# A transformer chain in split fp32: high and low parts of x side by side in the column chunks, and the first two chunks of five stages with token tiles stationary

## What is computed

```python
x = layer_norm(ALPHA * x + dsa_mixer(x))             # sparse attention
x = layer_norm(ALPHA * x + squared_relu_mlp(x))      # jnp.square(relu(x @ w_up)) @ w_down, 1024 -> 4096
x = layer_norm(ALPHA * x + gla_mixer(x))             # q, k, v, r, a_low = split(x @ w_in); 4 heads
x = layer_norm(ALPHA * x + squared_relu_mlp(x))
x = layer_norm(ALPHA * x + mla_mixer(x))             # latents = x @ w_dqkv first
x = layer_norm(ALPHA * x + swiglu_ffn(x))            # (silu(g) * u) @ w_down, 1024 -> 2 x 2816
x = x + sigmoid(x @ ple_w_gate) * (p[0] @ ple_w_proj)
x = layer_norm(ALPHA * x + hgrn2_mixer(x))           # q, f, v, gate = split(x @ w_in); 8 heads
x = layer_norm(ALPHA * x + swiglu_ffn(x))
x = x + sigmoid(x @ ple_w_gate) * (p[1] @ ple_w_proj)
# layer_norm: (x - mean) * rsqrt(mean((x - mean)**2) + 1e-5) * g + b
# gla_mixer: log_a = log_sigmoid(a_low @ w_a2 + b_a) / 16 decays the state, q and k are scaled by it
```

## Time and profile before

| | us |
|---|---|
| median of 3 runs | 1422.44 |
| lowest, highest | 1420.70, 1422.44 |
| the profiled execution | 1421.68 |
| its span (first to last instruction) | 1419.9 |
| TensorE busy in it | 1311.9 (92%) |
| VectorE, ScalarE busy | 843.4 (59%), 572.2 (40%) |
| mean granted TensorE clock, as a share of full rate | 0.967 |

### The profile page before, as it was taken

One profiled execution on the slowest core, in us unless ns is written; L12 is line 12 of the kernel. 1 busy time (PEld: TensorE's weight loads), 2 busy tenths in 40 slices (PEclk: granted clock), 3 DMA queues, 4 the chain that ended last, 5 costly groups with the idle time before them and its releaser, 6 DMA issues.

```text
span 1419.9 us, 19097 instructions
## 1 busy us (share of the span) xinstructions
PE 1311.9 (92%) x8181; PEld 1185.4 (83%) x8181; DVE 843.4 (59%) x1146; ACT 572.2 (40%) x652; POOL 82.6 (6%) x198
## 2 busy tenths in 40 slices
PE   6978899997998899999878899999999988999997
PEld 5867799996987799997767899998898877999996
DVE  5584855557566755557645754447667658554465
ACT  5452344443633344443342433444451233433333
POOL 2450000000000000000230000000000000000000
PEclk9999999999999999999889999999999999999999
DMA  7410655554632455554330655555553325555542
GB/s 247 147 60 2 207 178 185 198 181 145 189 129 90 156 197 181 185 198 144 119 119 8 226 190 178 185 195 191 172 164 119 119 67 178 180 192 192 179 152 86
DMA packets 128757, 221.06 MB, mean 156 GB/s; under 512 B 6904, under 2 KB 97040, under 8 KB 128672
## 3 DMA queue, kind: packets, MB, share of 16 engines
q1 hardware_dynamic: 125648, 209.83, 44.1%
q0 software_dynamic: 3024, 10.01, 2.4%
HBM read 218.77 MB, written 1.05 MB: 155 GB/s over the span
## 4 chain that ended last, share of the span: by engine, by line
PE 80%; DVE 12%; ACT 4%; DMA 3%; issue 1%; POOL 0%; SPq 0%; ACTq 0%; POOLq 0%
PE ps L499 18%; PE ps L476 18%; PE ps L477 18%; PE ps L478 17%; PE ps L745 2%; DVE wlo L1354 2%; PE ps L584 2%; DVE y L1429 2%; DVE stats L1400 1%; PE ps L597 1%; DVE y L1397 1%; DVE x L1432 1%; ACT whi L1008 1%; ACT buf L1076 1%; PE ps L713 1%
## 5 line engine op out<-in xcount | busy, mean ns | idle before, releaser
L1354 DVE TENSOR_TENSOR wlo<-raw,whi 128x2048 fp32r<-128x2048 f32 (+2 forms) x201 | 454.0, 2265 | 259.1 <-ACT whi L1008 258.8
L1008 ACT ACTIVATE whi<-raw 128x2048 fp32r<-128x2048 f32 (+2 forms) x201 | 377.9, 1886 | 172.2 <-DMA raw<-in_mlp_w_down 46.5
L476 PE MATMUL ps<-xh,whi 128*128 128x256 f32 x1400 | 398.5, 285 | 6.1 <-ACT buf L1270 2.4
L477 PE MATMUL ps<-xh,wlo 128*128 128x256 f32 x1400 | 397.9, 284 | 0.0
L478 PE MATMUL ps<-xl,whi 128*128 128x256 f32 x1400 | 397.7, 284 | 0.0
L476 PEld LDWEIGHTS ps<-xh,whi 128*128 128x128 f32 x1400 | 270.3, 193 | 9.3 <-issue 5.0
L477 PEld LDWEIGHTS ps<-xh,wlo 128*128 128x128 f32 x1400 | 270.3, 193 | 1.6
L478 PEld LDWEIGHTS ps<-xl,whi 128*128 128x128 f32 x1400 | 270.2, 193 | 0.0
L476 PE MATMUL ps<-whi,hh 128*128 128x512 f32 x432 | 168.7, 390 | 0.0
L477 PE MATMUL ps<-whi,hl 128*128 128x512 f32 x432 | 168.6, 390 | 0.0
L478 PE MATMUL ps<-wlo,hh 128*128 128x512 f32 x432 | 168.1, 389 | 0.0
(11 more groups left out here) (281 smaller groups left out, 1101.8 us busy)
## 6 DMA issues: line engine op xcount, KB each, us to landing
raw<-in_ffn_w_in SPq DMA_DIRECT2D x44, 1024.0 KB, 5.1
raw<-in_mlp_w_up SPq DMA_DIRECT2D x32, 1024.0 KB, 5.4
raw<-in_mlp_w_down SPq DMA_DIRECT2D x32, 1024.0 KB, 4.9
raw<-in_ffn_w_down SPq DMA_DIRECT2D x22, 1024.0 KB, 4.8
raw<-in_hgrn_w_in SPq DMA_DIRECT2D x16, 1024.0 KB, 5.4
raw<-in_b_w_in SPq DMA_DIRECT2D x12, 1024.0 KB, 5.3
raw<-in_a_w_in SPq DMA_DIRECT2D x8, 1024.0 KB, 7.2
raw<-in_ple_w_gate SPq DMA_DIRECT2D x8, 1024.0 KB, 6.0
```

The costliest lines, as they stand in the source:

```text
L476: mm(o, a[0], b[0], start=start, stop=False)
L477: mm(o, a[1], b[0], start=False, stop=False)
L1008: a.activation(whi[:, slot, 0:w], raw[:, slot, 0:w], ACT.Copy).then_inc(s["hi_done"], 1)
L1354: v.tensor_tensor(wlo[:, slot, 0:w], raw[:, slot, 0:w], whi[:, slot, 0:w].bitcast(F32), ALU.subtract).then_inc(s["lo_done"], 1)
```

## The change

**Side by side.** `xh` and `xl` become two halves of one tile `xhl[:, kk, 2, 256]`. In a column chunk each (f, kk) is now one matmul of 512 moving columns (high weight by high and low x at once) and one of 256 (low weight by high x). Group f fills its own PSUM bank, b + f; its two halves are partial sums, which VectorE adds with `sum_parts`, a `tensor_reduce` over pairs that lie 256 apart (L1529 after), into SBUF. ScalarE and VectorE take what they read from PSUM before (silu's and relu's input, f, q, k) from there. A chunk waits for the sum before last (`summed`) before it takes its banks again.

**First two chunks.** At T_X1, T_X2, T_X3, T_X5 and T_X8 `first_two` takes the place of `turn_to_columns` and of the chunk behind it: both chunks with token tile 0 stationary (2 x 24 matmuls of 256 columns) as soon as tile 0 is turned, and again with tile 1. ScalarE copies each 128 x 256 result to SBUF (`rows_copy`, into `staged`, which is the buffer `work`), and TensorE transposes it back (`turn_rows`). 

**Before the norm.** `by_halves`: the first weight chunk of tile 1 does both column halves first, the others half 0, then half 1, and tile 0 of the next stage's x is turned ahead of the last part. The norm sums the residual with `accum_out` in the same pass, ScalarE squares (`squares`, two passes of 512 with the mean as bias and `accum_out`), `gain` is one pass per half and comes ahead of the root, and the splits of the next chunks and of tile 0 stand ahead of the sum of tile 1's second half.

**The rest.** In the MLP VectorE makes relu and square in one (`max, mult`) and ScalarE copies it rounded. GLA's order is q0, q1, low-rank gate, k0 (with the gate logits inside), k1. HGRN's sigmoids and silus read the sums. T_X4's tile 0 is turned earlier too.

```diff
-            def columns(w, o, f0=0):
-                for f in range(f0, 2):
+            def columns(n, b, within=None):
+                k = column_no[n]
+                if k >= 2:
+                    pe.wait_ge(s["summed"], k - 1)
+                take(n)
+                w = weights(n, KD, FG)
+                for f in range(2):
+                    if f == 1 and within:
+                        within()
                     for kk in range(KD):
-                        last = three(o[:, 256 * f : 256 * f + 256], [v[:, kk, P * f : P * f + P] for v in w],
-                                     [v[:, kk, :] for v in (xh, xl)], kk == 0, kk == KD - 1)
+                        mm(bank(b + f), w[0][:, kk, P * f : P * f + P], xhl[:, kk, :, :].rearrange("p a n -> p (a n)"), start=(kk == 0), stop=False)
+                        last = mm(bank(b + f, 256), w[1][:, kk, P * f : P * f + P], xh[:, kk, :], start=False, stop=(kk == KD - 1))
+            def sum_parts(n, b, dst):
+                dve.wait_ge(s["w_done"], n + 1)
+                v.tensor_reduce(dst, ps[:, b : b + 2, :].rearrange("p f (a n) -> p f n a", a=2), AX_X, ALU.add).then_inc(s["summed"], 1)
+            def first_two(j, n):
+                b = ROWS_AT[j]
+                out = lambda i, tt: ps[:, i + 2 * tt, 0:256]
+                take(n)
+                rows_chunk(j, n, 0, out(0, 0)).then_inc(s["rows_done"], 1)
+                take(n + 1)
+                rows_chunk(j, n + 1, 0, out(1, 0), 1, lambda: turn_tile(j, x, 1)).then_inc(s["rows_done"], 1)
+                rows_chunk(j, n, 1, out(0, 1)).then_inc(s["w_done"], 1)
+                rows_chunk(j, n + 1, 1, out(1, 1), 0, lambda: turn_rows(b, 0)).then_inc(s["w_done"], 1)
+            def turn_rows(b, i):
+                pe.wait_ge(s["rows_out"], 4 * b + 3 + i)
...
+            def by_halves(j, first_parts, held, half):
+                for c in range(2):
+                    for q, (n, part) in enumerate(held):
+                        if c == 0 and q == 0:
+                            for n0, part0 in first_parts:
+                                part0(0)
+                                part0(1).then_inc(s["w_done"], 1)
+                        if j is not None and c == 1 and q == len(held) - 1:
+                            turn_tile(j, x, 0)
+                        last = part(c)
...
+            def normed(i, n_last, j):
+                squares(i, 0)
+                ahead(n_last - 1)
+                turned_tile(j, 0)
+                squares(i, 1)
+                if j in ROWS_AT:
+                    rows_copy(j, n_last, 0, 0)
+                turned_tile(j, 1)
+                if j in ROWS_AT:
+                    rows_copy(j, n_last, 1, 0)
+                    rows_copy(j, n_last, 0, 1)
...
@@ ScalarE, mlp @@
-                    ahead(up(g))
-                    act.wait_ge(s["w_done"], up(g) + 1)
-                    a.activation(r, bank(0 if g == 0 else 4 + g % 3), ACT.Relu).then_inc(s["h_act"], 1)
-                    act.wait_ge(s["h_act"], hcount(layer, 0, g) + 1)
-                    a.activation(hh[:, slot, :], r, ACT.Square).then_inc(s["h_hi"], 1)
+                    if g > 0:
+                        ahead(up(g))
+                    if g < 2:
+                        act.wait_ge(s["rows_turned"], 2 * ROWS_AT[j] + g + 1)
+                        a.activation(r, bank(6 + g), ACT.Relu).then_inc(s["h_act"], 1)
+                    if g == 0:
+                        rows_copy(j, up(0) - 1, 1, 1)
+                        ahead(up(0) - 1)
+                    act.wait_ge(s["h_full"], MLP_GROUPS * layer + g + 1)
+                    a.activation(hh[:, slot, :], buf[2][:, 512 * slot : 512 * slot + 512], ACT.Copy).then_inc(s["h_hi"], 1)
@@ VectorE, layer_norm @@
+                sums(0, 0)
+                sums(0, 1)
+                normal(0)
                 dve.wait_ge(s["half_done"], i + 1)
                 sums(1, 0)
-                sums(1, 2)
+                if not beside:
+                    ahead(n_last - 1)
+                    turned(j, 0)
                 dve.wait_ge(s["w_done"], n_last + 1)
                 sums(1, 1)
-                sums(1, 3)
-                root(1, between_second)
+                normal(1)
@@ VectorE, GLA @@
             ahead(first["gla_low"])
-            for q in range(4):
-                ahead(first["gla_qk"] + q)
+            for q in range(2):
+                ahead(first["gla_k"] + q)
+                sum_parts(first["gla_k"] + q, 2 - 2 * q, k4[0][:, 2 * q : 2 * q + 2, :])
             dve.wait_ge(s["tail_done"], 1)
```

More of the change, by code:

```diff
@@ L544, in square, with by_tile, part @@
                     by_rows(n0 + q, 2, D, 2 * q, KD, wide(base))
-            def by_tile(j, src, n0, done, half, side=None):
+            def by_tile(j, src, n0, done, half, j_next, side=None):
+                def part(q, c):
+                    return rows(n0 + q, 2, D, 2 * q, KD, wide(0)[2 + c : 3 + c], operand=(j, 1))
                 if side is not None:
@@ L574, in turn_to_columns @@
-            def turn_to_columns(j, n, o):
+                if j_next is None:
+                    for c in range(2):
+                        for q in range(4):
+                            last = part(q, c)
+                            if c == 0 and q == 3:
+                                last.then_inc(s[half], 1)
+                            if c == 1:
+                                last.then_inc(s["w_done"], 1)
+                else:
+                    by_halves(j_next, [(n0, lambda c: part(0, c))], [(n0 + q, lambda c, q=q: part(q, c)) for q in range(1, 4)], half)
@@ new lines, in rows_chunk @@
+            def rows_chunk(j, n, tt, o, at=None, within=None):
+                w = weights(n, KD, FG)
+                for step, (part, w_part) in enumerate(((0, 0), (0, 1), (1, 0))):
+                    for kk in range(KD):
+                        if step != 1 and kk % (KD // 2) == 0:
+                            operand_ready(j, tt, kk // (KD // 2), part)
+                        last = mm(o, (xh, xl)[part][:, kk, P * tt : P * tt + P], w[w_part][:, kk, :],
+                                  start=(step == 0 and kk == 0), stop=(step == 2 and kk == KD - 1))
+                    if step == at:
+                        within()
+                return last
@@ L576, in turn_to_columns @@
+            def turn_to_columns(j, n, b):
                 for tt in range(TT):
                     turn_tile(j, x, tt)
[L578 to L585 removed]
@@ L1108, in ple @@
                 n0 = first[f"ple{layer}"]
+                for tt in range(TT):
+                    squares(5 + 2 * layer, tt)
                 for u in range(4):
@@ new lines, in _ @@
+            act.wait_ge(s["rows_turned"], 2 * ROWS_AT[T_X2] + 2)
+            projected(1)
+            ahead(first["gla_q"] + 1)
+            act.wait_ge(s["gates"], 1)
+            for h in range(4):
+                last = a.activation(expo[0][:, 256 * h : 256 * h + 256], ps[:, 6 + h // 2, 256 * (h % 2) : 256 * (h % 2) + 256],
+                                    ACT.Identity, bias=vcol[:, V_BA + h : V_BA + h + 1])
+            step(last)
+            step(a.activation(expo[1], expo[0], ACT.Abs))
@@ L1221, in _ @@
+            step(a.activation(expo[1], expo[1], ACT.Exp, scale=-1.0))
+            a.activation(expo[1], expo[1], ACT.Ln, bias=1.0).then_inc(s["tail_done"], 1)
+            for q in range(2):
+                ahead(first["gla_k"] + q)
             act.wait_ge(s["gate_logs"], 1)
```

389 lines of the change are left out of this document (190 added, 199 removed).

## The result

| | before | after |
|---|---|---|
| median, us | 1422.44 (4 runs) | 1445.40 (4 runs) |
| lowest, highest | 1420.70, 1422.90 | 1442.95, 1446.98 |
| profiled execution, its span | 1421.68, 1419.9 | 1442.95, 1441.2 |
| mean granted clock | 0.967 | 0.959 |

The changed kernel is slower by a factor of 1.0162, 95% interval 1.0144 to 1.0181. The forecast was 1425 with a range of 1410 to 1438, so it was too low by 20 us. The span grew by 21.3 us.

A forecast was written before the change was run, and what follows sets the result against it. It took TensorE's matmul stream as the bound inside feed-forward stages, and its waits elsewhere. Merge savings of 14.2 us and costs at the starts, GLA and HGRN summed to +2.6 on 1421.7: 1424.3, 1425 as median, range 1410 to 1438.

The forecast's parts named there:

- HGRN step: HGRN: first chunk waits for all low parts, +1.2 us; first q pair's sum comes after gates and tree, +1.4.
- merge, 76 chunks: Column chunks: one 512-column matmul replacing two of 256 saves 0.187 us a chunk, 14.2 us in all; bounds 7.6 and 15.7.
- first MLP's start: First feed-forward stage: first down chunk starts 1.9 us later, plus 1.75 for half clock after a 6 us gap: +3.6.
- second MLP's start: Second feed-forward stage: start 1.2 us later with a 3.0 us norm gap, plus two clock falls of 1.75: +4.7 us.
- gated starts: Two gated stages: 1.5 us saved, 1.75 lost to half clock after a 3.8 us gap, +0.3; the other, +2.1.
- GLA to the first decay step: GLA: k's high part behind a copy, v's pair sum behind low parts, 8.9 us idle ahead of v: +9.2 us.
- latents: X4: low parts go ahead of the norm's last sum, so tile 1's rows start at 677.2 instead of 681.2: -4.0 us.
- norms beside the side projection: The two norms end 0.9 us earlier and TensorE's 1.6 us wait shrinks by that: -1.7 us.
- Rival (a): The five starts are covered after all, their waits of 31.7 us and clock falls gone: 1361 us; chance 0.07.
- Rival (c): VectorE's pair sum, inputs 256 apart, costs twice 1.22 us and lands on the path: 1433 us; chance 0.18.
- Rival (b): TensorE's clock stays up in the new gaps, sparing 8 falls of 1.75 us: 1411 us; chance 0.15.

The follow-up runs named there:

- first_split_only: `early_splits` with only the first of its two moves, the second chunk's high part staying behind the last copy: 1414.94 us, ratio 0.9968 to the kernel before.
- early_splits: Changed kernel with ScalarE making the next two weight chunks' high parts ahead of row-result copies at the five starts: 1412.21 us, ratio 0.9934 to the kernel before.
- sum_twice: `early_splits` with every pair sum of the feed-forward stages made twice on VectorE: 1450.10 us, ratio 1.0192 to the kernel before.
- hgrn_order: Changed kernel with HGRN's VectorE queue reordered, sums ahead of low parts and of gates and tree: 1435.39 us, ratio 1.0100 to the kernel before.

## Why the prediction was wrong, step by step

In short: the queues at the starts were foreseen. What failed were the HGRN step, which left one low part out of VectorE's queue and the second wait out altogether, and the size of the merge. Measured from start to start in the two profiles; a plus is time that the change costs. The 8 merged chunks of HGRN are in the first line, so their 0.9 us are taken out of HGRN's. The stretch of the first MLP, for instance, is 140.91 to 178.57 before (the start in the earlier trace rows, the end of the first down chunk) and 139.81 to 181.72 after.

| step | predicted | measured |
|---|---|---|
| merge, 76 chunks | -14.2 | -8.4 |
| first MLP's start | +3.6 | +4.3 |
| second MLP's start | +4.7 | +4.8 |
| gated starts | +0.3, +2.1 | +1.6, +2.7 |
| GLA to the first decay step | +9.2 | +11.4 |
| latents | -4.0 | -3.1 |
| norms beside the side projection | -1.7 | +0.4 |
| HGRN | +2.6 | +10.3 |
| sum | +2.6 | +24.0 |

The span grew by 21.3. The rest is -1.1 us ahead of 140 and -1.5 in the second attention, where nothing was meant to change. The median lies 2.5 us above the profiled execution (0.8 before). Single executions differ by several us in stretches that hold the same code, so a step is known no closer than that from one pair of profiles: HGRN, for one, is 3.9 us shorter in the profile of `first_split_only` than in that of `early_splits`.

**Right: the queues at the starts.** The mechanism at the four feed-forward starts came out as worked out, the sizes within 1.3 us (13.4 us in all, forecast 10.7). At the gated ones the half rate behind the wait cost 2.6 us and not 1.75: two column chunks took 13.90 us, against 11.28. The text put the first down chunk at 174.9, with TensorE idle from 169.0; it started at 174.33 after 5.46 us. The norm gap was to shrink to 2.4 us and is 2.56; the total of these gaps was put at about 12 us and is 11.3 (13.9 less three waits of 1.18, 1.18 and 0.26 for other tiles). `early_splits` shows the cause: the order alone moves 33 us, 7 of them in GLA. Rival (a), the starts covered after all, did not happen. With those two lines elsewhere its picture of the starts holds, but not its 1361 us: the 11.3 us under the norms stay, and no run of any kernel here came under 1395.

**Right: the pair sum.** 78 sums take 1222 ns each, where the row gave 1220. Rival (c) did not happen. `sum_twice` shows that its reasoning was sound on the held groups and too mild on the price.

**Wrong in size: the merge, 5.8 us.** The step took the mean of 24 matmuls of 512 columns in a row (227.9 ns) for a 512 that stands between two of 256. The pair takes 352.5 ns, where 227.9 and 119.8 give 347.7. The text had this as its lower bound, a lone 512 that takes 5 ns more, and took 14.2, near the other one. (That bound is 76 x 16 x 6.7 ns = 8.1 us, not 7.6.) A pitch held for the sequence it was read in, and even there not always: in HGRN two chunks in a row took 11.09 us in the changed kernel (1038.32 to 1049.41), 346.5 ns a pair, and 11.31 in `hgrn_order`, 353.4 ns. No run looks for why.

**Wrong: HGRN, 7.7 us.** The step named the sum behind gates and tree and put it 12.4 us after the end of the f chunk, 1.4 us too late for TensorE (12.4 less 11.1 is 1.3). The list of seven durations was right, but it began too early. When the f chunk ends, VectorE first makes a low part, and the f chunk's sum starts behind it at 1046.13. From VectorE's timeline, the low part, that sum, and the late one behind gates and tree:

```profile
1043.92 2.29 DVE L1431 TENSOR_TENSOR wlo<-raw,whi 128x2048 fp32r<-128x2048 f32 x1 [3.16 <-ACT whi L1049]
1046.13 1.22 DVE L1529 TENSOR_REDUCE buf<-ps 128x512 f32<-128x1024 f32 x1
...
1057.40 1.22 DVE L1529 TENSOR_REDUCE buf<-ps 128x512 f32<-128x1024 f32 x1
```

That is the missing 2.2 us of the 3.56, and the half rate behind it costs 1.65 more. The 3.53 us ahead of the first decay step was not seen at all: a low part and the sum of an f chunk stand ahead of the masked copy (L1681). The kernel before waits there for 1.62 us, so 1.9 us are new, and the half rate behind them costs 1.2. That makes 6.9 of the 7.7 us. `hgrn_order` took 10 us back with the order alone.

**Wrong in size: GLA, 2.2 us, and the side norms, 2.1.** In GLA the forecast was 8.9 us idle ahead of v, and it is 8.34. But the first k chunk started 1.0 us later than put (once the 1.5 us are taken off by which this execution is later at the norm), the two k chunks took 1.3 us longer, and the v chunk 0.5. The side norms were to save 0.9 us each. Instead TensorE's waits there are 1.11 us for ScalarE's turned tile and 1.17 for VectorE's low part, where it was 0.34 and 1.60 before; no run here looks for the cause.

The mean granted clock tells the same in one number (0.967 to 0.959). Rival (b), the clock stays up in the new gaps, is out: behind six of the eight waits shown above the first matmul took twice its 0.39 us, and behind a seventh 0.66. Of the four norm gaps the ones of 2.56 and 2.39 us were not followed by half rate and those of 2.71 and 2.73 were. The prediction took a fall for the two it had at 3.0 and none for the two at 2.4, so it had the four right, at 1.75 us a fall. From the turning through tile 1's first 40 matmuls it is 5.95 us at the first gated start, without a fall, and 7.28 and 6.99 us with one: a fall cost 1.3 and 1.0 us. The length of a gap alone does not decide, though: in the kernel before, the wait of 1.62 us at 1058.52 was followed by a granted clock of 0.56 between 1060 and 1062.

## What to carry to other kernels

When a change hides work under a wait, write down for each other engine what stands in its queue behind the new instructions, for the whole stretch up to the next steady loop. Here ScalarE was idle for six of the eight microseconds in which the split could have been made, and two lines decided between 1445 and 1412 us. And look at the last groups of a loop apart from the loop: VectorE had room for a second sum in the steady groups, and none where the groups are held back.

## What the runs showed of the hardware

A matmul of 512 columns costs 227.9 ns in a run of its kind and some 232.7 between two of 256 in the feed-forward stages, so that high and low part side by side save 6.9 ns of 359.4 in each contraction step, 2%. A reduce over pairs that lie 256 elements apart in PSUM takes 1222 ns for 1024 elements, as much as the one over neighbours in the earlier trace rows (1220).
